# Hymba decoder trunk: a copy moved between the halves of a task's exponentials, and half a tile finished on ScalarE and GpSimd

## What is computed

```python
for l in range(DEPTH):                       # DEPTH = 2
    proj = jnp.einsum('btd,dn->btn', x, w_in[l])
    ...
    # mixer A, for each block of 128 queries:
    def probs(q, k):
        sc = jnp.einsum('bhqd,bhkd->bhqk', qb, k) * scale
        return jax.nn.softmax(jnp.where(mask, sc, -jnp.inf), axis=-1)
    p = probs(q1, k1) - lam * probs(q2, k2)
    o = jnp.einsum('bhqk,bhkd->bhqd', p, v)
    ...
    x = layer_norm(ALPHA * x + mix, ln1_g[l], ln1_b[l])
    hid = jnp.square(jax.nn.relu(jnp.einsum('btd,df->btf', x, w_up[l])))
    x = layer_norm(ALPHA * x + jnp.einsum('btf,fd->btd', hid, w_down[l]), ln2_g[l], ln2_b[l])
return x
```

## Time and profile before

| | |
|---|---|
| median of 3 runs | 1256.25 us (1255.68 to 1256.77) |
| profiled execution, its own time | 1256.2 us |
| its span | 1254.4 us |
| PE busy | 1235.6 us, 98% |
| DVE, ACT, POOL busy | 725.2, 477.3, 488.9 us |
| DMA | 110.28 MB, mean 88 GB/s |
| granted TensorE clock | 0.999 |

### The profile page before, as it was taken

The page is one execution under the profiler, slowest core; times in us unless marked ns, Lnnn a source line. Parts: engine busy times, 40 slices in busy tenths (PEclk is TensorE's granted clock), DMA queues, the critical chain, the costliest instruction groups (busy, mean ns, idle before and its releaser), DMA issues.

```text
span 1254.4 us, 18654 instructions
## 1 busy us (share of the span) xinstructions
PE 1235.6 (98%) x7514; PEld 1026.6 (82%) x7514; DVE 725.2 (58%) x1120; ACT 477.3 (38%) x946; POOL 488.9 (39%) x277
## 2 busy tenths in 40 slices
PE   8999999999999999999999999999999999999997
PEld 8998666789888888888899976668988888888885
DVE  4396778369672262360397867783797623605406
ACT  5326678623222231222143366784333322222210
POOL 1468000044444444444345760003264444444442
PEclk9999999999999999999999999999999999999999
DMA  7533001132522322232224320013233332233211
GB/s 254 134 75 102 2 1 52 51 106 97 172 91 95 101 101 94 92 101 97 63 59 128 94 69 1 19 35 106 79 135 100 101 101 91 95 101 101 93 59 67
DMA packets 77973, 110.28 MB, mean 88 GB/s; under 512 B 17664, under 2 KB 38336, under 8 KB 77760
## 3 DMA queue, kind: packets, MB, share of 16 engines
q1 hardware_dynamic: 76304, 104.31, 26.4%
q10 hardware_dynamic: 1584, 4.78, 1.1%
HBM read 106.98 MB, written 2.10 MB: 87 GB/s over the span
## 4 chain that ended last, share of the span: by engine, by line
PE 91%; DVE 4%; ACT 2%; issue 1%; POOL 1%; DMA 0%; DVEq 0%; ACTq 0%; POOLq 0%
PE ps L683 17%; PE ps L685 16%; PE ps L684 16%; PE ps L679 9%; PE ps L680 9%; PE ps L681 9%; PE ps L788 3%; PE ps L776 2%; PE ps L825 2%; PE ps L638 1%; PE ps L810 1%; ACT probs_a L1169 1%; DVE negmax L1432 1%; DVE probs_a L1485 1%; PE ps L901 1%
## 5 line engine op out<-in xcount | busy, mean ns | idle before, releaser
L549 POOL TENSOR_TENSOR w_lo<-raw,w_hi 128x1024 fp32r<-128x1024 f32 (+3 forms) x182 | 420.9, 2319 | 645.2 <-ACT w_hi L1041 644.7
L1041 ACT ACTIVATE w_hi<-raw 128x1024 fp32r<-128x1024 f32 (+3 forms) x200 | 198.6, 995 | 593.2 <-PE ps L685 361.9
L679 PE MATMUL ps<-xt_hi,w_lo 128*128 128x512 f32 (+1 forms) x576 | 210.7, 366 | 0.0
L680 PE MATMUL ps<-xt_hi,w_hi 128*128 128x512 f32 (+1 forms) x576 | 210.5, 366 | 0.0
L681 PE MATMUL ps<-xt_lo,w_hi 128*128 128x512 f32 (+1 forms) x576 | 210.5, 365 | 0.0
L683 PE MATMUL ps<-w_hi,xt_lo 128*128 128x384 f32 (+3 forms) x448 | 152.5, 340 | 0.6 <-DVE xt_lo L1277 0.3
L683 PE MATMUL ps<-w_hi,mt_lo 128*128 128x512 f32 x384 | 150.5, 392 | 0.2
L684 PE MATMUL ps<-w_hi,mt_hi 128*128 128x512 f32 x384 | 149.5, 389 | 0.0
L685 PE MATMUL ps<-w_lo,mt_hi 128*128 128x512 f32 x384 | 149.4, 389 | 0.0
L685 PE MATMUL ps<-w_lo,xt_hi 128*128 128x384 f32 (+3 forms) x448 | 148.0, 330 | 0.0
L684 PE MATMUL ps<-w_hi,xt_hi 128*128 128x384 f32 (+3 forms) x448 | 148.0, 330 | 0.0
(11 more groups left out here) (175 smaller groups left out, 1865.8 us busy)
## 6 DMA issues: line engine op xcount, KB each, us to landing
raw<-in_w_up SPq DMA_DIRECT2D x64, 512.0 KB, 3.4
raw<-in_w_down SPq DMA_DIRECT2D x64, 512.0 KB, 3.8
raw<-in_w_in SPq DMA_DIRECT2D x32, 384.0 KB, 3.2
raw<-in_w_in SPq DMA_DIRECT2D x16, 256.0 KB, 2.8
raw<-in_w_in SPq DMA_DIRECT2D x32, 128.0 KB, 2.5
raw<-in_w_out SPq DMA_DIRECT2D x8, 512.0 KB, 3.2
raw<-in_w_out SPq DMA_DIRECT2D x12, 256.0 KB, 3.7
rows<-in_ln_g ACTq DMA_DIRECT2D x4, 512.0 KB, 3.9
```

The costliest lines, as they stand in the source:

```text
L549: nc.gpsimd.tensor_tensor(unit_of(w_lo, u), unit_of(raw, u), unit_of(w_hi, u).bitcast(F32), ALU.subtract).then_inc(s_lo_ready, 1)
L679: mm(o, wl[:, c], a_hi[:, k, cols], start=first, stop=False)
L680: mm(o, wh[:, c], a_hi[:, k, cols], start=False, stop=False)
L1041: A(unit_of(w_hi, u), unit_of(raw, u), ACT.Copy).then_inc(s_hi_ready, 1)
```

## The change

It has two parts.

**The copy.** On ACT, for t = 2, 4, 6 and 8 in each layer, `copy_p(t - 1)` no longer stands behind all exponentials of task t but between the first half of its parts and the second half. The number of instructions is the same.

**The last tiles.** Of tile 2's `scale_and_shift`, DVE does columns 0 to 511 alone. Columns 512 to 1023 are multiplied by the reciprocal deviation on ACT (one ACTIVATE, Identity) and get the bias row on POOL (one add). The stores are now: tiles 0 and 1 whole, tile 2's left half, tile 3's left half, tile 2's right half (waits for POOL), tile 3's right half: six in place of five.

```diff
@@ sync
-            for tt in range(3):
-                sp.wait_ge(s_out_last, tt + 1)
-                sp.dma_start(out[0, tt * P:(tt + 1) * P, :], xres[:, tt]).then_inc(s_stored, 16)
-            for half in range(2):
-                sp.wait_ge(s_out_last, 4 + half)
-                c = slice(512 * half, 512 * half + 512)
-                sp.dma_start(out[0, 3 * P:4 * P, c], xres[:, 3, c]).then_inc(s_stored, 16)
-            sp.wait_ge(s_stored, 16 * (TT + 1))
+            for n, (tt, c, w) in enumerate(((0, 0, D), (1, 0, D), (2, 0, 512), (3, 0, 512))):
+                sp.wait_ge(s_out_last, n + 1)
+                sp.dma_start(out[0, tt * P:(tt + 1) * P, c:c + w], xres[:, tt, c:c + w]).then_inc(s_stored, 16)
+            sp.wait_ge(s_out_third, 1)
+            sp.dma_start(out[0, 2 * P:3 * P, 512:D], xres[:, 2, 512:D]).then_inc(s_stored, 16)
+            sp.wait_ge(s_out_last, 5)
+            sp.dma_start(out[0, 3 * P:4 * P, 512:D], xres[:, 3, 512:D]).then_inc(s_stored, 16)
+            sp.wait_ge(s_stored, 16 * (TT + 2))
@@ gpsimd
                 rstd_of(layer, 1)
+                if layer == DEPTH - 1:
+                    pool.wait_ge(s_third_scaled, 1)
+                    nc.gpsimd.tensor_tensor(xres[:, 2, 512:D], xres[:, 2, 512:D], rows[:, 1, 512:D], ALU.add).then_inc(s_out_third, 1)
@@ scalar
-                def exps(t):
+                def exps(t, between=None):
...
-                    for a, _, _, n, at_ in task(t)[1]:
-                        for hh in range(2):
-                            last = A(probs_of(t)[:, hh, at_:at_ + n], ps[:, 2 * (t % 2) + hh, at_:at_ + n], ACT.Exp,
-                                     bias=negmax[:, t % 2, a, hh:hh + 1], accum_out=sums[:, t % 4, a, hh:hh + 1])
+                    parts = [(a, n, at_, hh) for a, _, _, n, at_ in task(t)[1] for hh in range(2)]
+                    for e, (a, n, at_, hh) in enumerate(parts):
+                        if between and 2 * e == len(parts):
+                            between()
+                        last = A(probs_of(t)[:, hh, at_:at_ + n], ps[:, 2 * (t % 2) + hh, at_:at_ + n], ACT.Exp,
+                                 bias=negmax[:, t % 2, a, hh:hh + 1], accum_out=sums[:, t % 4, a, hh:hh + 1])
                     last.then_inc(s_exped, 1)
...
                 for t in range(TASKS):
+                    among = 2 <= t < 2 * BOTH - 2 and t % 2 == 0
                     if t >= 2:
-                        exps(t)
+                        exps(t, (lambda: copy_p(t - 1)) if among else None)
...
-                    if t and turns(t - 1):
+                    if t and turns(t - 1) and not among:
                         copy_p(t - 1)
...
+            act.wait_ge(s_rstd, nth("rstd", DEPTH - 1, 2 * TT - 1))
+            act.wait_ge(s_out_centred, 3)
+            A(xres[:, 2, 512:D], xres[:, 2, 512:D], ACT.Identity, scale=rstd[:, 2:3], bias=lams[:, 6:7]).then_inc(s_third_scaled, 1)
@@ vector
-                def scale_and_shift(tt, parts=1):
+                def scale_and_shift(tt, parts=1, end=D):
...
-                    for c in range(0, D, n):
+                    for c in range(0, end, n):
...
-                    scale_and_shift(2)
+                    scale_and_shift(2, 2, 512)
                     scale_and_shift(3, 2)
```

More of the change, by code:

```diff
@@ L375, in build @@
         s_out_last = sem("out_last")
+        s_out_third = sem("out_third")
+        s_third_scaled = sem("third_scaled")
         s_oa_squared = sem("oa_squared")
```

## The result

The changed kernel takes 1258.0 us (median of 20 runs, 1257.15 to 1258.65), the kernel before in the same comparison 1255.83 us (20 runs, 1255.4 to 1256.77): a ratio of 1.0015, 95% interval 1.0009 to 1.0021. That is 2.2 us slower, where +2.4 was forecast. The profiled span went from 1254.4 to 1256.4 us.

A forecast was written before the change was run, and what follows sets the result against it. PE was taken as the bound, 91% of the chain. Copies at +0.98 us per layer, twice +1.96, plus +0.45 for the tail gave +2.4 us, 1258.6 us, with a range of 1256.2 to 1259.9.

The forecast's parts named there:

- Task 2: ACT's moved copy at task 2, while PE is busy with the last input chunk: cost and gain 0.
- Task 4: Exponentials end 0.97 us later, but POOL's rotation holds DVE anyway, so DVE's weights end only 0.45 later.
- Rival 1: Full delay at task 4, 0.97 instead of 0.45: +1.5 us per layer, +3.5 in all, 1259.7; chance 0.17.
- Task 6: Earlier copy lets PE start the values of task 5 0.46 us earlier; not carried to the scores of task 12.
- Task 8: `exped` comes 0.98 us later, and so do task 10's exponentials and PE's scores of task 12, in each layer.
- rival 2: DVE's factors at task 9 slip past POOL's subtraction: up to 1.1 us per layer back, 1256.3; chance 0.13.
- The tail: Last tiles: POOL's add and DVE exclude each other, so the last stores end at 1254.6: +0.45 us.
- Rival 3: No exclusion between POOL and DVE in the tail: -0.5 us there, 1257.7 in all; chance 0.12.
- The sum: Whole kernel: 1.96 us for the copies in two layers plus 0.45 for the tail, +2.4 us, 1258.6.
- Rival 4: Copy pays if DVE has slack at tasks 4 and 8: PE keeps up to 0.7 us per layer, 1254.3; chance 0.08.
- The signs that the prediction named: Trace: values of task 5 0.5 us earlier, task 8's reciprocal and task 12's scores 1 later, one tail instruction over 1.2.

The follow-up runs named there:

- e12: Kernel before with only the copy of task 1 moved, into task 2, tail as before: 1256.03 us, ratio 0.9998.
- e3: Kernel before with only the copy of task 3 moved, into task 4, tail as before: 1256.89 us, ratio 1.0005.
- e5: Kernel before with only the copy of task 7 moved, into task 8, tail as before: 1258.59 us, ratio 1.0018.
- e9: Kernel before with the copies of tasks 5 and 7 moved, into tasks 6 and 8, tail as before: 1256.63 us, ratio 1.0003.
- e2: Changed kernel with the copies taken back, so only the tail is changed: 1256.52 us, ratio 1.0005.
- e6: Changed tail alone, copies as before, without POOL's add; the half's store waits for ScalarE's multiplication: 1255.79 us, ratio 0.9996.
- e1: Changed kernel with the tail of before, so only the four copies are moved: 1257.02 us, ratio 1.0009.

## Why the prediction was right, point by point

- **Task 2: 0.** Right: 0.02 in the stretch and at most 0.02 before it (e12).
- **Task 4: the exponentials of task 6 start 0.45 late, not 0.97, because POOL's rotation covers DVE.** Right: 129.66 in place of 129.12, less the start's 0.17, is 0.37. DVE's two instructions took 0.86 and 0.47 us in place of 1.02 and 0.95 (the earlier trace rows have the second), and the one that was held ended 0.29 after POOL's rotation in both kernels (125.70 after 125.41; 125.57 after 125.28). e3, where nothing else is moved, ends with +0.34. Rival 1 is out, though no run takes POOL's rotation away.
- **Task 6: the values of task 5 start 0.46 earlier, and nothing of it is carried on.** 0.38 on the profile's clock, 0.55 without the start's shift; the idle time fell from 0.71 to 0.17. That it is carried away was right in the changed kernel. What the prediction missed is that being early pays at task 8, where it spares ACT a wait of 0.55 us for the turn (e5 against e9). The prediction had that wait in its times for the kernel as changed, so its sum was not touched, but I did not see that the copies depend on each other, and the expectation of e5 failed on it.
- **Task 8: `exped` 0.98 late, and all of it arrives.** The first half was right within about 0.1: 0.87, as the first part of task 8 started 0.17 late and not 0.3. The second was too strict, and this is the term that was mis-sized, 0.98 against 0.61 and 0.70. The rest went where rival 2 had put it, in small: the reciprocal of task 9 no longer waited for ACT, the factors started at 142.06, 0.04 us ahead of POOL's subtraction at 142.10, and took 0.16 in place of 1.32. Then POOL got in, as the rival's own "against" had it, and the first of the two L1497 behind was held instead: 1.48, ending 0.41 after POOL's 143.58, in place of 0.62. Of 1.1 us that could have come back, 0.2 to 0.3 did.
- **The tail: +0.45.** +0.47 in the changed kernel, +0.53 in e2. POOL's add took 1.40, not 1.2, and the half of tile 3 ended 0.55 after it, where 0.6 was taken. The mechanism was right, but that the number came so near is in part luck, because the prediction's own terms don't give it: stores that begin at 1251.2 and take 3.4 end at 1254.6, and against 1254.0 that is +0.6. Taken back by 1.53, the time by which the last centring starts later, they began at 1251.12 and the last landed 3.35 later, at 1254.47. Rival 3, no exclusion, is out: e6 gives what it would have been, -0.52, where the forecast had -0.5.
- **The sum.** 1.96 + 0.45 = 2.4 forecast; 1.31 + 0.47 = 1.8 in the profile, 2.2 in the medians, and the ratio of 1.0015 is 1.9 us. e1 has 1.43 for the copies. So the term of the copies was 0.5 to 0.65 us too large, and the medians, which hold the scatter of the start too, stand nearer to the forecast than the places that it was added up from.
- **Rival 4, the copy pays.** It decides at DVE's idle time before the reciprocals of tasks 4 and 8, and that idle time grew, from 0.39 and 0.44 to 1.37 and 1.14 us, with ACT named each time. Out.

The signs that the prediction named are all there: the values of task 5 0.55 earlier with 0.17 of idle time before them, the reciprocal of task 8 0.87 later with 1.14, the scores of task 12 0.61 later with PE idle, 0.69 in layer 1, and one instruction of 1.75 beside POOL's add.

What the Trainium skill says on its page SBUF — State Buffer, section "SBUF: two separate sides", that a VectorE instruction with two SBUF inputs and a GpSimd instruction that reads SBUF block each other for its whole length, this case bears out: 1.75 us with POOL's add beside it, 0.75 without (e6). One GpSimd instruction of the tail doesn't show it; it stands in the last section.

## What to carry to other kernels

When a copy is put before half of the work it used to follow, look at who waits for the second half: here one wait of TensorE shrank by 0.5 us and the waits behind a chain over VectorE grew by more, because the idle time of TensorE at one task was only the first of two limits. The gain came from the second, by taking a reduction that nobody needed yet, the GpSimd instruction that it sets off and the exponential behind that out of the way. And before work in a tail is given to another engine, check that it shares nothing with the engine it relieves, and whether the tail isn't bound by transfers that could simply start sooner.

## What the runs showed of the hardware

- VectorE and GpSimd took turns in three places read here: each time GpSimd came in behind the VectorE instruction then running, before the next in VectorE's queue (before, 141.07 ahead of the factors at 141.24; changed, 142.10 after the factors at 142.06; in the tail GpSimd's add, started at 1250.67, before the second half at 1250.87). One place doesn't fit: GpSimd's reciprocal of one number per partition, 1247.65 to 1249.17, ended 0.42 us after VectorE's L1337, and yet VectorE's next instruction, started at 1248.68, took 1.28 as it does with no GpSimd beside it. Why is open. The VectorE instruction that is held ends 0.55 us after GpSimd's for 128x512 with two inputs, where alone it takes 0.75.
- An add of 128x512 float32 on GpSimd takes 1.40 us beside VectorE, a multiplication of 128x512 on ScalarE with a per-partition factor and bias 0.81:

```profile
1247.78 0.81 ACT L1270 ACTIVATE xres<-xres,lams,rstd 128x512 f32<-128x512 f32 x1 [21.32 <-POOL rstd L558]
```

- Moves of 0.3 us and less on hand-written queues can be read from a profile though not from the median: the stretch of 28.5 us repeated within 0.05 us over two layers and five kernels that leave it alone, while the start of the program moved by up to 1.6 us between executions.
